# A hybrid attention and recurrence layer: both units' gate products and the scores of two blocks in one stretch of 64-row products behind the first recurrent gate's tile

## The reference, cut to what matters

```
h = RMSNorm(x); z = h @ W_in          # q 1024 | k 256 | v 256 | attention gate 1024 | recurrent input 1024 | recurrent gate 1024
attention: 16 query heads, 4 key/value heads of 64, window of 128, banded blocks of 128, a sink per head
    p = exp(scores - m) / (sum + exp(sink - m));  o = p @ v
recurrence: u = causal conv of width 4 over its input
    r, i = sigmoid(u @ W_r + b_r), sigmoid(u @ W_i + b_i)   # 16 diagonal blocks of 64 x 64
    a = exp(-8 r softplus(-lam));  h_t = a h_(t-1) + sqrt(1 - a^2) (i u)
y = concat(RMSNorm(o * silu(gate_a)), RMSNorm(h * silu(gate_l)));  out = RMSNorm(x + y @ W_out)
```

## Time and profile before

| | |
|---|---|
| median of 3 runs | 1382.4 us (1381.16 to 1384.33) |
| the profiled execution, its own time | 1383.39 us |
| its span, first to last instruction | 1381.8 us |
| PE busy | 1359.5 us, 98% of the span |
| DVE busy | 954.0 us, 69% |
| ACT busy | 819.0 us, 59% |
| POOL busy | 192.7 us, 14% |
| mean granted TensorE clock | 0.997 |

### The profile page before, as it was taken

The page is one execution under the profiler, slowest core; times in us unless marked ns, Lnnn a source line. Parts: engine busy times, 40 slices in busy tenths (PEclk is TensorE's granted clock), DMA queues, the critical chain, the costliest instruction groups (busy, mean ns, idle before and its releaser), DMA issues.

```text
span 1381.8 us, 22240 instructions
## 1 busy us (share of the span) xinstructions
PE 1359.5 (98%) x6746; PEld 1109.0 (80%) x6746; DVE 954.0 (69%) x1663; ACT 819.0 (59%) x1695; POOL 192.7 (14%) x251
## 2 busy tenths in 40 slices
PE   8999999999999999999999999999999999999998
PEld 7787877788888888888888888888877888888886
DVE  6898989868686777778687767777686534444442
ACT  7869687857767575757767485766764321213120
POOL 2020212112030212112030211112020000000000
PEclk9999999999999999999999999999999999999999
DMA  8685858654545546363545565454635423233220
GB/s 315 212 276 197 309 201 269 249 191 164 194 169 187 193 166 230 141 214 141 212 159 212 177 233 192 153 187 171 214 115 176 151 76 106 93 89 109 73 92 31
DMA packets 98290, 243.22 MB, mean 176 GB/s; under 512 B 8113, under 2 KB 43057, under 8 KB 98225
## 3 DMA queue, kind: packets, MB, share of 16 engines
q1 hardware_dynamic: 91200, 217.79, 46.1%
q0 software_dynamic: 7024, 24.65, 4.7%
HBM read 179.49 MB, written 62.91 MB: 175 GB/s over the span
## 4 chain that ended last, share of the span: by engine, by line
PE 79%; ACT 8%; DVE 7%; issue 4%; DMA 1%; ACTq 0%; DVEq 0%; SPq 0%
PE ring L1492 44%; PE acc_b L204 13%; PE ring L204 11%; PE ps_s L1525 3%; PE ps_v L1546 3%; PE ring L1559 2%; ACT p_sb L851 1%; PE ps_t L1533 1%; ACT w_hi L711 1%; DVE hs L1334 1%; DVE w_lo L1039 1%; DVE o_sb L1266 1%; DMA w_raw<-w_out_d 1%; PE ring L1569 1%; DVE ya L1274 1%
## 5 line engine op out<-in xcount | busy, mean ns | idle before, releaser
L1492 PE MATMUL ring<-split,w_hi 128*128 128x512 f32 x2288 | 717.5, 395 | 3.9 <-DVE w_lo L1039 2.8
L1492 PEld LDWEIGHTS ring<-split,w_hi 128*128 128x128 f32 x2288 | 421.1, 188 | 100.3 <-issue 6.9
L1492 PE MATMUL ring<-split,w_lo 128*128 128x512 f32 x1144 | 446.8, 391 | 0.0
L1492 PEld LDWEIGHTS ring<-split,w_lo 128*128 128x128 f32 x1144 | 214.7, 188 | 46.1
L637 POOL TENSOR_SCALAR_AFFINE_SELECT p_hi_c<-p_hi 128x512 fp32r<-128x512 f32 x64 | 41.1, 642 | 707.5 <-ACT p_hi L859 707.5
L1291 DVE SCALAR_TENSOR_TENSOR cu<-xl,prm,cu 128x512 f32<-128x512 f32 x96 | 72.0, 750 | 48.1 <-ACT cu L878 43.2
L851 ACT ACTIVATE p_sb<-s_sb,smax 128x129 f32<-128x129 f32 x256 | 99.5, 391 | 0.6
L1770 ACT ACTIVATE w_hi<-res 128x1024 fp32r<-128x1024 f32 x15 | 15.9, 1061 | 134.4 <-DVE res L1840 134.4
L204 PE MATMUL acc_b<-wo_rest,y_own 128*128 128x512 f32 x384 | 91.3, 395 | 1.8 <-DVE wo_rest L165 1.8
L204 PE MATMUL ring<-split,y_own 128*128 128x512 f32 x384 | 91.4, 393 | 0.5 <-DVE split L165 0.5
L204 PEld LDWEIGHTS acc_b<-wo_rest,y_own 128*128 128x128 f32 x384 | 72.8, 190 | 17.8 <-DVE wo_rest L165 2.5
(11 more groups left out here) (240 smaller groups left out, 2382.5 us busy)
## 6 DMA issues: line engine op xcount, KB each, us to landing
w_hi<-w_split_scratch SPq DMA_DIRECT2D x108, 512.0 KB, 3.3
...
```

The lines of the kernel that those rows point to most:

```text
L1492: last = mm(bank(r), w[:, i % WSLOTS, k, :], h[:, par, k, :], start=(k == 0 and j == 0), stop=(k == KC - 1 and j == 2))
```

## The change

It moves work on all four engines and changes some buffers.

- **PE**: `gates(0)`, `score(0)`, `score(1)`, `gates(1)` stand in one run of 64-row products behind projection GL0. Before, `score(0)` and `gates(0)` stood behind XL1, and `gates(1)` and `score(1)` behind GL0. `turn_p(b)` and `weigh_v(b)` come one projection later, so `weigh_v(3)` stands behind Q1. Seven warming products at the start become twelve.
- **Buffers**: the second block's scores go into the two banks of `ps_t` and `ps_v` (one tensor `ps_tv` now), which nothing else uses at that place. `score(1)` waits for the last reader of those banks in the iteration before, `turn_p(0)` for `select(1)`. The high and low part of unit 1's `cu` go into `p_hi` and `p_lo`, so each unit has its own. GL0 comes before R0 and I0 in the ring.
- **ACT**: `take_r` and `take_i` become `take_gates`, four halves in a row, with the first tanh of the decay apart as `first_decay`. `take_gates(0)` stands ahead of `s_copy(0)`.
- **DVE and POOL** follow the new order.

```diff
-(R_XL0, R_XL1, R_R0, R_I0, R_GL0, R_R1, R_I1, R_GA0, R_GA1, R_XT0, R_XT1, R_GL1, R_KV, R_Q0, R_Q1,
+(R_XL0, R_XL1, R_GL0, R_R0, R_I0, R_R1, R_I1, R_GA0, R_GA1, R_XT0, R_XT1, R_GL1, R_KV, R_Q0, R_Q1,
...
+
+        by_token = lambda w: w[:, :, :].rearrange("p h t -> p (h t)")
+        u_parts = [(u_hi[:, :], u_lo[:, :]), (by_token(p_hi), by_token(p_lo))]
...
-        ps_t = ctx.enter_context(nc.psum_tensor("ps_t", [P, GQ, BLK], F32))
-        ps_v = ctx.enter_context(nc.psum_tensor("ps_v", [P, GQ, BLK], F32))
+
+        ps_tv = ctx.enter_context(nc.psum_tensor("ps_tv", [P, 2, T], F32))
+        ps_t, ps_v = (ps_tv[:, i, :].rearrange("p (h t) -> p h t", h=GQ) for i in range(2))
+        ps_second = ps_tv[:, :, :].rearrange("p i (h c) -> p (i h) c", h=2)
+        scores_of = lambda b: ps_second if b == 1 else ps_s
...
                 p_current(n, 0)
+                lru_gate(n, 0)
                 p_current(n, 1)
-                lru_gate(n, 0)
                 p_current(n, 2)
-                p_current(n, 3)
                 if not last:
                     if nxt_par != par:
                         pool.wait_ge(table_in, (q + 2) * 32)
                     sine_k(n)
+                p_current(n, 3)
+                if not last:
                     sine_q(n, 0)
                 write_out(n, g, q)
...
-                    act.wait_ge(*ring_ready.at(n, R_I0 + 1 if u else R_I1 + 1 - NR))
-                    nc.scalar.activation(u_hi[:, :], cu[u][:, :], ACT.Copy).then_inc(*u_high.one())
+                    act.wait_ge(*(pv.at(n, 0) if u else ring_ready.at(n, R_I0 + 1 - NR)))
+                    nc.scalar.activation(u_parts[u][0], cu[u][:, :], ACT.Copy).then_inc(*u_high.one())
...
-                def take_r(u):
+                def take_gates(u):
+
                     G = g * UNITS + u
                     act.wait_ge(*ring_ready.at(n, R_I[u] + 1))
                     act.wait_ge(*scanned.at(n, u + 1 - UNITS))
                     act.sem_inc(settled, 1)
-                    for to, r in ((lower, R_R[u]), (upper, R_I[u])):
+                    for to, r, rows in ((lower, R_R[u], upper), (upper, R_I[u], lower)):
                         nc.scalar.activation(ra[u][to, :], bank(r)[to, :], ACT.Tanh, scale=0.5,
                                              bias=prm[to, C_BR, bass.ds(G, 1)]).then_inc(*gate_r.one())
+                        nc.scalar.activation(ri[u][to, :], bank(r)[rows, :], ACT.Tanh, scale=0.5,
+                                             bias=prm[to, C_BI, bass.ds(G, 1)]).then_inc(*ring_act.one())
+
+                def first_decay(u):
+                    G = g * UNITS + u
                     act.wait_ge(*gate_r.at(n, 2 * u + 2))
                     act.wait_ge(*yl_out[u].at(n, 0))
                     act.sem_inc(settled, 1)
                     nc.scalar.activation(hs[u][:, :], ra[u][:, :], ACT.Tanh, scale=prm[:, C_POS4SP, bass.ds(G, 1)],
                                          bias=prm[:, C_POS4SP, bass.ds(G, 1)]).then_inc(*decay.one())
-
-                def take_i(u):
-                    G = g * UNITS + u
-                    act.sem_inc(settled, 1)
-                    for to, r, rows in ((lower, R_R[u], upper), (upper, R_I[u], lower)):
-                        nc.scalar.activation(ri[u][to, :], bank(r)[rows, :], ACT.Tanh, scale=0.5,
-                                             bias=prm[to, C_BI, bass.ds(G, 1)]).then_inc(*ring_act.one())
...
@@ -947,36 +953,34 @@
                     proj.high_w(act, 2 * g - 4)
                 high_u(0)
                 lru_in(1)
-                s_copy(0)
-                take_r(0)
-                high_u(1)
-                take_i(0)
-                high_dv(n)
                 if split:
                     split_w(n, GA1)
+                high_dv(n)
+                high_u(1)
+                gate_l(0)
+                take_gates(0)
+                s_copy(0)
+                s_copy(1)
+                first_decay(0)
+                take_gates(1)
+                decays(0)
+                if split:
+                    split_w(n, GL1)
                 s_exp(0)
-                gate_l(0)
-                decays(0)
-                s_copy(1)
-                take_r(1)
+                first_decay(1)
                 decays(1)
+                gate_a(0)
+                s_copy(2)
                 s_exp(1)
-                high_p(0)
-                s_copy(2)
-                take_i(1)
-                gate_a(0)
                 if q < NQUART - 1:
                     root_x(n, x_ms.at(n, 1), x_root)
                 lru_root(0)
                 lru_root(1)
-                if split:
-                    split_w(n, GL1)
                 if split_next:
                     split_w(n, KVG)
                 s_exp(2)
+                high_p(0)
                 gate_a(1)
-                high_p(1)
-                low_o(0)
                 s_copy(3)
                 if q < NQUART - 1:
                     for half in range(2):
@@ -984,27 +988,27 @@
                                ring_ready.at(n, R_XT0 + half + 1), h_high.one())
                 elif g > 1:
                     proj.high_w(act, 2 * g - 3)
-                high_p(2)
-                low_o(1)
-                if last:
-
-                    act.wait_ge(*ring_ready.at(n, R_GA1 + 1))
-                s_exp(3)
                 if split_next:
                     split_w(n, Q0)
                 gate_l(1)
+                low_o(0)
+                high_p(1)
                 if last:
+
+                    act.wait_ge(*ring_ready.at(n, R_GA1 + 1))
                     proj.high_y(act, 0, 1)
...
+                s_exp(3)
+                if last:
                     proj.high_w(act, 5)
                 if split_next:
...
-                low_o(2)
-                high_p(3)
+                low_o(1)
+                high_p(2)
...
+                low_o(2)
+                high_p(3)
                 if split_next:
                     split_w(n, NG + XL1)
                 if not last:
                     high_q(n, 0)
                     take_q(n, 1)
+                low_o(3)
+                if not last:
...
-                conv(1)
-                select(0)
-                low_u(1)
-                top(0)
-                differ_v(n)
                 if split:
                     split_w(n, GA0)
-                low_v(n, g)
-                softmax_b(0)
+                differ_v(n)
+                conv(1)
+                low_u(1)
                 silu_l(0)
                 if split:
                     split_w(n, GA1)
-                one_less(0)
-                input_x(0)
+                low_v(n, g)
+                select(0)
+                top(0)
                 select(1)
                 top(1)
+                input_x(0)
+                one_less(0)
+                if split:
+                    split_w(n, GL1)
+                softmax_b(0)
+                input_x(1)
+                silu_a(0)
                 one_less(1)
-                softmax_b(1)
-                low_p(0)
                 select(2)
                 top(2)
-                input_x(1)
-                silu_a(0)
+                softmax_b(1)
                 if q < NQUART - 1:
                     norm_x(n, x_root.at(n, 1), x_rs, x_norm)
                 lru_tail(0)
-                if split:
-                    split_w(n, GL1)
                 lru_scan(0)
                 if split_next:
                     split_w(n, KVG)
+                low_p(0)
                 softmax_b(2)
-                low_p(1)
-                add_o(0)
                 silu_a(1)
                 select(3)
                 top(3)
@@ -1392,40 +1397,38 @@
                               h_high.at(n, half + 1), ring_dve.one())
                 elif g > 1:
                     proj.low_w(dve, 2 * g - 3)
-                low_p(2)
-                gate_o(0)
-                add_o(1)
-                softmax_b(3)
                 if split_next:
                     split_w(n, Q0)
...
-            warm(7)
+            warm(12)
...
-                    pe.wait_ge(*s_sel.at(n, b))
+                    if b == 1:
+
+                        pe.wait_ge(*p_low.at(n, 0))
+                        pe.wait_ge(*o_sum.at(n, 0))
+                    else:
+
+                        pe.wait_ge(*s_sel.at(n, (0, None, 1, 3)[b]))
...
+                    if b == 0:
+
+                        pe.wait_ge(*s_sel.at(n, 2))
...
 
                 project(n, XL0, par, split)
                 project(n, XL1, par, split)
+                project(n, GL0, par, split)
+
+                gates(0)
                 score(0)
-                gates(0)
-                project(n, GL0, par, split)
+                score(1)
                 gates(1)
-                score(1)
                 project(n, GA0, par, split)
-                turn_p(0)
                 score(2)
                 project(n, GA1, par, split)
-                weigh_v(0)
-                turn_p(1)
```

(16 more changed lines are left out.)

43 lines of the change are left out of this document (24 added, 19 removed).

## The result

The changed kernel takes 1449.84 us (median of four, 1447.91 to 1450.79), the kernel before 1382.56: a ratio of 1.0484 [1.0466, 1.0502], 4.8% slower. Predicted were 1432 us and a range of 1405 to 1448, so the direction was right and the loss was underrated by 18 us, 1.8 beyond the range.

The account below looks back on a forecast made before the run. PE, busy 98% of the span, was taken to bound the kernel. Waits of 21 + 15 + 3 = +39 us gave 1421.4 on the median's scale; +11 for the clock made 1432 us, range 1405 to 1448.

Parts of the forecast that it names:

- term 2: Eight iterations of quarters 1 and 2: 3.0 us idle for late x less 0.40 saved, +2.6 each, +21 us.
- term 3: Quarter 0's four iterations: late x plus a wait of GL0 for its low part, 3.8 each, +15 us (12 to 18).
- term 4: Quarter 3: scores 3 still wait, +0.5 an iteration, up to 1 us more in its last two; +3 us (0 to 6).
- falls of the clock: PE's clock drops to 1.2 GHz behind long waits, 1.8 us lost each; 6 or 7 falls taken, +11 us.
- Term 1: On PE, one run of 64-row products fewer per iteration, saving 0.40 us each: -6.4 us over 16, included in the other terms.
- The chain of x: ACT's queue from take_gates(0) to the table load, 15.7 us, then root and norm_x; x ready at 450.2, PE asking at 447.2.
- The table load: ACT's table load ahead of x's root: 1.28 us with no drain, against the skill's 2.66.
- I take half: Of twelve iterations waiting for x, 6 or 7 bring a clock fall of 1.8 us, +11; all, with GL0's, would be 27.
- the wait without the clock: Rival: idle time of about 2 us does not lower PE's clock, so the waits stand alone, 1421 us; chance 0.28.
- Half the wait: Rival: ACT's chain 1 to 2 us shorter an iteration and no clock fall, 1406 down to 1397 us; chance 0.10.
- faster: Rival: x is ready before PE asks, so only the saved runs of 64-row products count, 1375 us; chance 0.12.
- Behind `turn_x` nothing else waits: On PE after x's transposes: the next product of p by v comes six microseconds later, so no further wait costed.

Follow-up runs that it names:

- run 2: Changed kernel with nine extra 512-column products ahead of turn_x's wait for x's norm, result overwritten: 1435.73 us, ratio 1.0383.
- run 9: run 8 with low_o(2), p's parts and add_o(2) ahead of q's first rotation, and quarter 0's gate_l(0), silu_l(0) and two splits moved: 1402.1 us.
- run 3: Changed kernel with four extra 512-column products ahead of turn_x's wait for x's norm: 1433.26 us, ratio 1.0365.
- run 6: Changed kernel with DVE's split of GL0's weights ahead of the first convolution in quarter 0: 1446.04 us, ratio 1.046.
- run 5: Kernel before the change, with three unused copies on ACT ahead of x's root in quarters 0 to 2, making x late: 1424.6 us, ratio 1.0304.
- run 1: Changed kernel with x's root on ACT ahead of unit 1's high part and x's norm on DVE right behind low_v: 1433.03 us, ratio 1.0363.
- run 7: Changed kernel with the moves of run 1 and run 6, select(2) sooner, add_o(0), low_p(1) and high_p(0) earlier: 1428.02 us, ratio 1.0331.
- run 8: run 7 with sine_k, gate_a(1), silu_a(1), x's mean and root earlier, and quarter 0's split of GA0 later: 1407.15 us, ratio 1.0174.

## Why the prediction was right and where it failed

The span grew by 67.4 us, where the forecast's terms add up to 50. Stretch by stretch, with what run 2 says of the clock:

| | forecast | measured |
|---|---|---|
| term 2, waits in quarters 1 and 2 | +21 | 515.16 - 494.82 = +20.3 |
| term 3, quarter 0's four iterations | +15 (12 to 18) | +24.6 with their falls, 280.96 - 257.34 = +23.6 with the two left in run 2 |
| term 4, quarter 3 and the end | +3 (0 to 6) | +7.3 |
| falls of the clock | +11 (0 to 27) | 17.1 in quarters 1 and 2, about 1 in quarter 0: +18 |
| start of the first iteration | not in the sum | -2.0 |

- *Term 1*, 0.40 saved by each merged run: right. The stretch took 3.02, and with all waits gone an iteration of quarter 1 is 0.51 shorter, one of quarter 3 0.67 (run 9). The 0.1 to 0.3 beyond it were not traced further. The rule of the Trainium skill that it was set beside (TensorEngine Tiling (Array Packing), Key Properties: changing the tiling mode drains TensorE) fits these rows; by that rule alone the change would have been faster, and the measurement went the other way, since the rule says nothing of what the new order makes late.
- *Term 2*, +2.6 in each of eight iterations: right to a tenth (64.43 against 61.84 in runs 2 and 3, where the clock stays up). The chain of x was 0.3 shorter than summed and began 0.2 later.
- *The table load*: 1.28 once more, with no idle time around it.
- *Term 3*: mis-sized, by 8.6 us. GL0 started 0.4 sooner than forecast (186.00 is 13.5 behind its iteration's first product; 175.04 of the earlier trace rows was 14.0 behind). But iteration 2 came out 7.0 longer and not 3.8: `turn_x` was 1.0 later than forecast, and behind it the clock, or without its fall DVE's tail, takes 1.5 or more. The forecast followed quarter 0 to `turn_x` alone and put nothing behind it. What makes that tail is shown only in part (run 6).
- *Term 4*: mis-sized, by 4.3 us. In quarter 3 `weigh_v(0)` waits for `low_p(0)` and its copy on GpSimd, 0.2 us each, and in the other quarters it does not, since `turn_x`'s wait comes first. Two of its iterations are 0.9 to 1.0 longer, not 0.5; the one ahead of the last is 2.5 longer (`weigh_v` waits 1.1 us there for `low_p(1)`, put at up to 1), and the last with phase B 2.9, though the 1.83 us of the earlier trace rows are two waits of 0.9 there (1110.73 and 1113.30) with no fall behind them.

**The mechanism was right; the steps that failed are three sizes: term 3, "I take half", and term 4.** Of the falls of the clock I took 6 or 7 at 1.8 us, +11; each of the twelve iterations with a wait for x had a fall, two more came behind GL0, and they are worth 18. The reason given for halving (the wait falls in another place than the one of phase B) had no row behind it, and the one row that there was the earlier trace rows spoke for a fall each time. Still, run 5 has the clock fall in only eight of twelve, so that all twelve would fall could not be known either. Of the 17 us that the span grew beyond the forecast's 50, term 3 has 8.6, the falls 7 and term 4 4.3, and the sooner start and term 2 give 2.7 back. The range shows the same: its upper end of 1448 is terms 2 to 4 at their centre and every fall at 1.8, so nothing was left in it for a term 3 or 4 that is too small, and both measured above their own ranges, while the falls stayed within theirs.

That the falls come from the waits and not from the merged run is shown from both sides: filling the idle time gave back 14 us with the wait for x still ending as late (run 2), and a late x in the kernel before brought falls without the change (run 5).

The rival *the wait without the clock* is nearest to run 3: 1433, where 1421 was given for it, and the 12 us between are terms 3 and 4 again. *Half the wait* and *faster* needed a shorter chain on ACT, and it was as long as summed.

"Behind `turn_x` nothing else waits" was right, and right only because of the delay: take it away and `low_p(1)`, `add_o(2)`, the rotation of k and, at a quarter's end, x's own parts are late one after another (runs 1, 7, 8, 9). Moving p's turns one projection on took slack from all of them.
